# Second mixer and end of a fused block: constants computed early, sums in one piece, a remainder moved, the last gate in smaller steps

## What is computed

```
for i in range(2):                       # layer 0: short convolution, layer 1: RG-LRU
    h = h + mixer_i(rmsnorm(h, norm_mix[i]))
    h = h + hier_moe(rmsnorm(h, norm_ffn[i]), ...)          # 32 experts, top 2
    gate = sigmoid(rmsnorm(h, norm_ple[i]) @ w_ple_gate[i] + b_ple_gate[i])
    h = h + gate * (p[i] @ w_ple[i])
return rmsnorm(h, norm_final)

def rglru_mixer(xn):                     # the second mixer
    y, u = split(xn @ w_in)              # in_y and in_b below
    u = depthwise_conv(u, conv_w) + conv_bias               # width 4
    r, i = sigmoid(u @ w_r + b_r), sigmoid(u @ w_i + b_i)   # "gates", blocks of 256, two directions
    log_a = -8 * r * softplus(-lam)      # softplus(-lam): the decay constants
    a = exp(log_a)
    h = scan(a, sqrt(-expm1(2 * log_a)) * i * u)            # forward, and backward
    return (gelu(y) * (h_forward + h_backward)) @ w_out
```

## Time and profile before

| | |
|---|---|
| median of 3 runs | 1695.89 us (1693.95 to 1697.94) |
| profiled execution | 1695.1 us, its span 1693.1 us |
| TensorE busy | 1364.1 us (81%) |
| VectorE busy | 590.7 us (35%) |
| ScalarE busy | 434.9 us (26%) |
| HBM | 525.91 MB read, 311 GB/s over the span |

### The profile page before, as it was taken

How to read it: one execution, slowest core, us unless ns; L and a number is a source line. 1 busy time by engine, 2 the same in 40 slices (tenths; PEclk the granted TensorE clock), 3 DMA queues, 4 the chain that set the end, 5 groups by cost and what they waited for, 6 DMA issues and landing times.

```text
span 1693.1 us, 21874 instructions
## 1 busy us (share of the span) xinstructions
PE 1364.1 (81%) x9534; PEld 899.0 (53%) x9534; DVE 590.7 (35%) x1136; ACT 434.9 (26%) x658; POOL 219.7 (13%) x119
## 2 busy tenths in 40 slices
PE   4999998999999996776567677989966767666677
PEld 2797797999989961222122123978622212221226
DVE  2576623899437620110110012677201001101115
ACT  3444334534453320000000002566200000000015
POOL 0307322487430000000000000000000000000000
PEclk9999889999999997887888789999988878878789
DMA  9314435344554979999999999538799999999991
GB/s 403 122 61 166 196 111 201 120 179 153 171 199 156 393 318 429 427 426 427 427 429 427 427 425 412 211 110 358 275 427 427 427 426 428 427 427 427 426 411 71
DMA packets 51760, 528.39 MB, mean 312 GB/s; under 512 B 4688, under 2 KB 4816, under 8 KB 19920
## 3 DMA queue, kind: packets, MB, share of 16 engines
q1 hardware_dynamic: 51088, 525.22, 75.9%
q10 hardware_dynamic: 576, 1.75, 0.3%
HBM read 525.91 MB, written 1.05 MB: 311 GB/s over the span
## 4 chain that ended last, share of the span: by engine, by line
PE 50%; DMA 38%; DVE 5%; SPq 3%; ACT 2%; issue 1%; POOL 0%; DVEq 0%; ACTq 0%; POOLq 0%
PE bank L617 24%; PE bank L1180 9%; DMA ring<-in_w_up 7%; DMA ring<-in_w_gate 7%; DMA ring<-in_w_down 7%; DMA work<-in_w_gate 7%; DMA work<-in_w_up 4%; DMA work<-in_w_down 3%; PE bank L1200 3%; PE bank L1257 2%; SPq L518 2%; DMA ring<-in_dense 2%; PE bank L1326 2%; PE bank L610 1%; PE bank L689 1%; PE bank L1049 1%
## 5 line engine op out<-in xcount | busy, mean ns | idle before, releaser
L1180 PE MATMUL bank<-ring,work 128*32 128x512 f32 x1216 | 272.0, 731 | 141.4 <-DMA ring<-in_w_up 78.4
L617 PE MATMUL bank<-work_rounded,ring_rounded 128*128 128x256 f32 (+1 forms) x2032 | 317.5, 291 | 6.5 <-DVE xn_rounded L1940 3.5
L617 PEld LDWEIGHTS bank<-work_rounded,ring_rounded 128*128 128x128 f32 x2032 | 277.2, 190 | 16.1 <-issue 6.1
L617 PE MATMUL bank<-xn_rounded,ring_rounded 128*128 128x256 f32 (+1 forms) x1472 | 255.0, 291 | 3.4 <-DVE xn_rounded L1934 3.4
L1180 PEld LDWEIGHTS bank<-ring,work 128*32 128x32 f32 x1216 | 58.5, 130 | 319.6 <-issue 117.9
L617 PEld LDWEIGHTS bank<-xn_rounded,ring_rounded 128*128 128x128 f32 x1472 | 209.0, 194 | 7.7 <-issue 4.5
L2463 DVE TENSOR_TENSOR work<-work,bank 128x512 f32<-128x512 f32 x16 | 11.0, 687 | 569.5 <-PE bank L1180 569.5
L1835 POOL TENSOR_TENSOR ring_rounded<-ring,ring_rounded 128x2048 fp32r<-128x2048 f32 (+1 forms) x37 | 159.5, 4328 | 207.1 <-ACT ring_rounded L1394 207.1
L1180 PE MATMUL bank<-work 128*32 128x512 f32 x496 | 146.1, 698 | 33.6 <-DMA work<-in_w_gate 17.5
L1902 POOL TENSOR_TENSOR work<-work_rounded,work 128x128 f32<-128x128 f32 x32 | 12.1, 399 | 1079.2 <-PE bank L1232 738.4
L1394 ACT ACTIVATE ring_rounded<-ring 128x2048 fp32r<-128x2048 f32 (+1 forms) x78 | 136.5, 1795 | 46.3 <-PE bank L617 26.9
(11 more groups left out here) (329 smaller groups left out, 1718.0 us busy)
## 6 DMA issues: line engine op xcount, KB each, us to landing
ring<-in_dense SPq DMA_DIRECT2D x48, 2048.0 KB, 8.7
ring<-in_w_up SPq DMA_DIRECT2D x44, 2048.0 KB, 30.1
ring<-in_w_down SPq DMA_DIRECT2D x36, 2048.0 KB, 30.5
ring<-in_w_gate SPq DMA_DIRECT2D x32, 2048.0 KB, 29.8
work<-in_w_gate SPq DMA_DIRECT2D x16, 2048.0 KB, 23.1
work<-in_w_down SPq DMA_DIRECT2D x16, 2048.0 KB, 32.3
spare<-in_w_gate SPq DMA_DIRECT2D x8, 2048.0 KB, 28.9
work<-in_w_up SPq DMA_DIRECT2D x8, 2048.0 KB, 31.8
```

Of the source, the lines that this page charges most:

```text
L617: last = mm(out, rv(high_store[r][:, at:at + P]), rv(x[part][k]), start=opens and k == 0 and j == 0, stop=closes and k == n_k - 1 and j == 2)
L1180: ins = mm(out[slots(y), :], xg[:, k, slots(y)], expert_columns(w, at, 512), start=k == 0, stop=k == KT - 1)
```

## The change

1. The decay constants are computed at the start of the program, into a tensor of their own, with scratch in `small`.
2. In the second mixer the eight norm sums follow product k = 5 in one piece.
3. `weights_low(w_in_y)` for chunk 0 follows convolution block 3.
4. In the last layer the gate has five uses: three of two tiles, then tile 6 and tile 7 alone. VectorE prepares logits ahead; the last sums use a pairwise sum for tiles 0 to 3 and VectorE's square for tile 7; VectorE also scales tiles 5 to 7. The final multiply and store go in three parts (tiles 0 to 2, 3 to 5, 6 and 7).

```diff
+OUT_PARTS = ((0, 3), (3, 6), (6, 8))
-        ("out_b", 4), ("ple1", 4)]
+        ("out_b", 4), ("ple1", 5)]
+    rates = nc.alloc_sbuf_tensor("rates", [P, 16], F32)
+    def gate_tiles(layer, b):
+        return (2 * b, 2 * b + 2) if layer == 0 or b < 3 else (b + 3, b + 4)
-    nls = flat(17408, 16)
-    nlt = [flat(17424 + 16 * i, 16) for i in range(5)]
+    nls = rates[:]
+    nlt = [wk("small", 16, 16 * i) for i in range(5)]
...
@@ TensorE
             if k == 5:
-                sum_squares(range(4), h_sq)
-        sum_squares(range(4, KT), h_sq)
+                sum_squares(squared=h_sq)
...
-        sum_squares(squared=h_sq)
+        final = 4 * (count["norms"] + 1)
+        for k, sem, value in ((0, "sq_added", 3), (1, "sq_added", 3), (4, "sq_ready", final + 3), (5, "sq_ready", final + 3),
+                              (6, "sq_ready", final + 4), (7, "sq_added", 4)):
+            pe.wait_ge(S[sem], value)
+            last = mm(bank[4][:, 0:SEQ], ones, h_sq[:, k], start=k == 0, stop=k == KT - 1)
+        signal(last, "ss_ready")
@@ ScalarE, start
         high(w_abh, par("w_ab"))
+        act.wait_ge(S["lru_log"], 1)
+        signal(act.activation(nlt[1], nlt[1], ACT.Exp, scale=-1.0), "lru_exp")
@@ ScalarE, ple(1)
+            gate(0)
+            gate(1)
+            square(0)
+            normed(0, 1)
+            square(1)
+            gate(2)
+            normed(2, 3)
+            gate(3)
+            square(2)
+            square(3)
+            normed(4)
+            gate(4)
@@ ScalarE, second mixer
-        act.wait_ge(S["lru_log"], 1)
-        signal(act.activation(nlt[1], nlt[1], ACT.Exp, scale=-1.0), "lru_exp")
@@ VectorE, start
+        x = par("lam")
+        signal(v.scalar_tensor_tensor(nlt[1], x, -1.0, x, ALU.mult, ALU.max), "lru_log")
         low(par("w_ab"), w_abh, "dve_step")
+        dve.wait_ge(S["lru_exp"], 1)
+        log1p(nlt[2], nlt[1], nlt[3:5])
+        after(v.tensor_scalar(nlt[0], x, -1.0, 0.0, ALU.mult, ALU.max))
+        after(v.tensor_tensor(nlt[0], nlt[0], nlt[2], ALU.add))
+        signal(v.tensor_scalar(nls, nlt[0], -RG_C, None, ALU.mult), "lru_log")
+        dve.wait_ge(S["lru_log"], 2)
@@ VectorE, ple(1)
+            logits(0)
+            logits(1)
+            added(0)
+            added(1)
+            logits(2)
+            dve.wait_ge(S["sq_ready"], 4 * (7 + 3 * layer) + 2)
+            signal(v.tensor_tensor(h_sq[:, 0:2], h_sq[:, 0:2], h_sq[:, 2:4], ALU.add), "sq_added")
+            added(2)
+            logits(3)
+            added(3)
+            logits(4)
+            added(4)
+            dve.wait_ge(S["h_ready"], count["h_ready"])
+            signal(v.tensor_tensor(h_sq[:, 7], hT[:, 7], hT[:, 7], ALU.mult), "sq_added")
+            for k in range(5, KT):
+                last = v.tensor_scalar(weighted[:, k], hT[:, k], par("norm_final", k, 1), None, ALU.mult)
+            after(last)
@@ VectorE, second mixer: the operations of the start are gone from here, and
-            if b == 2:
-                weights_low(FIRST["w_in_y"])
+        weights_low(FIRST["w_in_y"])
@@ VectorE, end
-        for half in range(2):
-            part = slice(4 * half, 4 * half + 4)
+        for a, e in OUT_PARTS:
```

More of the change, by code:

```diff
@@ L584, in _ @@
                 sp.dma_start(ring[SLOT[n]][:, a:b], t["dense"][seen][:, a:b]).then_inc(S[full], 16)
-        for half in range(2):
-            part = slice(4 * half, 4 * half + 4)
-            sp.wait_ge(S["fin_ready"], half + 1)
-            sp.dma_start(t["out"][:, part], yT[:, part]).then_inc(S["out_store"], 16)
-        sp.wait_ge(S["out_store"], 32)
+        for i, (a, e) in enumerate(OUT_PARTS):
+            sp.wait_ge(S["fin_ready"], i + 1)
+            sp.dma_start(t["out"][:, a:e], yT[:, a:e]).then_inc(S["out_store"], 16)
+        sp.wait_ge(S["out_store"], 16 * len(OUT_PARTS))
     @block.tensor
@@ L1283, in ple @@
             ready = next_input()
-            for b in range(2, 4):
-                dense_split(use + b, [(n + 1, (2 * b + i) % 4) for i in range(2)],
+            for b in range(2, 4 + layer):
+                dense_split(use + b, [(n + 1, j % 4) for j in range(*gate_tiles(layer, b))],
                             [[x[:, k] for k in range(KT)] for x in (ple_xh, xnT)], None if b > 2 else ready)
@@ L1743, in ple, with gate, square, normed @@
             functions(SIGMOID)
-            for b in range(4):
+            def gate(b):
                 released(act, USE[f"ple{layer}"] + b)
-                for x in range(2):
-                    j = 2 * b + x
+                for j in range(*gate_tiles(layer, b)):
                     last = act.activation(gsb[:, j], gsb[:, j], ACT.Sigmoid, bias=par("b_ple", 8 * layer + j, 1))
                 signal(last, "gate_ready")
-                pair = slice(2 * b, 2 * b + 2)
+            def square(b):
                 act.wait_ge(S["h_ready"], 16 + 4 * layer + b + 1)
-                if layer == 0:
+                tiles = slice(*gate_tiles(layer, b))
+                signal(act.activation(h_sq[:, tiles], hT[:, tiles], ACT.Square), "sq_ready")
+            def normed(*tiles):
+                for k in tiles:
+                    act.activation(weighted[:, k], hT[:, k], ACT.Identity, scale=par("norm_final", k, 1))
+            if layer == 0:
+                for b in range(4):
+                    gate(b)
+                    act.wait_ge(S["h_ready"], 16 + b + 1)
                     for k in (2 * b, 2 * b + 1):
                         signal(act.activation(in_b_x[:, k], hT[:, k], ACT.Identity, scale=par("norm_mix", 8 + k, 1)), "emb_ready")
[L1755 to L1760, removed]
+                    square(b)
+                    if b in (1, 2):
+                        split_half()
+                return
+            gate(0)
[10 more added lines that the diff above has]
+            gate(4)
         moe(0)
@@ L2492, in ple, with logits @@
             roots()
-            for b in range(4):
+            def logits(b):
                 n = USE[f"ple{layer}"] + b
                 x = full(n)
-                pair = slice(2 * b, 2 * b + 2)
-                g = gsb[:, pair]
-                free(v.tensor_tensor(g, x[:].rearrange("p (k t) -> p k t", k=2), rstd_sb.unsqueeze(1).to_broadcast([P, 2, SEQ]), ALU.mult), n)
-                dve.wait_ge(S["gate_ready"], 8 * layer + b + 1)
[L2500 to L2503, removed]
+                a, e = gate_tiles(layer, b)
+                free(v.tensor_tensor(gsb[:, a:e], x[:, 0:SEQ * (e - a)].rearrange("p (k t) -> p k t", k=e - a),
+                                     rstd_sb.unsqueeze(1).to_broadcast([P, e - a, SEQ]), ALU.mult), n)
@@ new lines, in added @@
+            def added(b):
+                a, e = gate_tiles(layer, b)
+                g = gsb[:, a:e]
+                dve.wait_ge(S["gate_ready"], 8 * layer + b + 1)
+                after(v.tensor_tensor(g, g, ple_y(layer, a // 2)[:, a % 2:a % 2 + e - a], ALU.mult))
+                signal(v.tensor_tensor(hT[:, a:e], hT[:, a:e], g, ALU.add), "h_ready")
+            if layer == 0:
+                for b in range(4):
+                    logits(b)
+                    added(b)
+                    if b == 2:
+                        weights_low(FIRST["w_in_b"] + 1, (0,))
+                return
@@ L2505, in _ @@
+            for k in range(5, KT):
+                last = v.tensor_scalar(weighted[:, k], hT[:, k], par("norm_final", k, 1), None, ALU.mult)
+            after(last)
         moe(0)
         ple(0)
-        x = par("lam")
-        signal(v.scalar_tensor_tensor(nlt[1], x, -1.0, x, ALU.mult, ALU.max), "lru_log")
         weights_low(FIRST["w_in_b"] + 1, (1,))
@@ L2511, in _ @@
             weighted_low(weighted[:, k], hT[:, k], par("norm_mix", 8 + k, 1), weighted_high[:, k])
[L2513 to L2518, removed]
         def divided(out, n):
@@ L2597, in _ @@
         roots()
-        for half in range(2):
-            part = slice(4 * half, 4 * half + 4)
-            signal(v.tensor_tensor(yT[:, part], weighted[:, part], rstd_sb.unsqueeze(1).to_broadcast([P, 4, SEQ]), ALU.mult),
+        for a, e in OUT_PARTS:
+            signal(v.tensor_tensor(yT[:, a:e], weighted[:, a:e], rstd_sb.unsqueeze(1).to_broadcast([P, e - a, SEQ]), ALU.mult),
                    "fin_ready")
```

## The result

The changed kernel takes 1682.8 us (median of 4 runs, 1682.01 to 1683.07), the kernel before 1695.66 (4 runs, 1693.95 to 1697.94). The ratio is 0.992, 95% interval 0.9908 to 0.9932: 12.9 us less, as far as the medians go. The forecast was 1682.6. The profiled execution took 1682.87 us, its span 1680.9 (before 1695.1 and 1693.1).

The account below looks back on a forecast made before the run. VectorE's sequence from the second mixer's norm to `divided` b = 3 was taken as the bound. Gains 8.5 + 4.4 = 12.9 us from 1695.1 gave 1682.2, forecast 1682.6; own range 1680.6 to 1685, wider range 1679.6 to 1687.4.

Parts of the forecast that it names:

- The bound and the gap: Second mixer: VectorE's sequence from norm to `divided` b = 3 bounds; TensorE stands 6.6 us in line 610.
- Constants, sums, remainder: Second mixer: VectorE path loses 3.7 us of constants, 1.6 by sums, 4.40 of `weights_low`; lead beyond the wait not paid out.
- The clock: TensorE behind the mixer's gap: granted clock 0.53 for 3.62 us; the dip counted as 1.9 us.
- The 8.5: Second mixer's gain in us, last gate product 1129.78 to 1121.27; 6.6 if the clock dips anyway.
- The expert layer: Expert layer 1: its DMA stream moves with TensorE and VectorE and stays as long; first refill near 1207.4.
- The last gate: End of the kernel: logits ahead and single last tiles gain 4.4 us, bounds 3.0 and 5.0.
- the sooner first store: End of the kernel: first of three stores goes after three tiles, 0.95 against 1.23, gaining 0.3 us.
- The rules weighed: Last gate: two Trainium skill rules spoke against it, leaving an estimated 3.8 us (table switch) or 2.4 us (third store).
- The gap that stays: Rival, second mixer: gap of 1 to 2 us and clock dip return; mixer gives 5 us, time 1686; chance 0.10.
- The swallowed gain: Rival, expert layer: DMA stream swallows the mixer's gain, only 4.4 us left, time 1690.7; chance 0.06.
- the idle last gate: Rival, end of the kernel: last gate gives nothing because its ScalarE queue is longer, time 1686.6; chance 0.05.
- The slower one: Rival, TensorE from 1130 to 1227: unbroken stretch granted only clock 0.81, 22.8 us more, time 1705; chance 0.03.

Follow-up runs that it names:

- filler: The kernel before plus 14 TensorE products of no use between gate products 2 and 3; ratio to before 0.9989 (0.998 to 0.9998).
- low_only_filled: low_only plus four TensorE products of no use in its gap of 2.19 us; 1690.17 us, one run.
- low_back: The changed kernel with `weights_low(w_in_y)` back between convolution blocks 2 and 3; ratio to the kernel before 0.9941 (0.9927 to 0.9954).
- mixer_only: The kernel before with the constants, sums and remainder edits, and the old last gate; ratio to before 0.9954 (0.9942 to 0.9966).
- pairs: The changed kernel with the last gate in four uses of two tiles, logits still prepared ahead; ratio to the kernel before 0.9943 (0.9924 to 0.9961).
- low_only: The kernel before with only `weights_low(w_in_y)` moved behind convolution block 3; ratio to before 0.9972 (0.9962 to 0.9982).
- gap_longer: low_back plus one VectorE operation of no use ahead of the divide of block 3; 1688.92 us, one run.
- tail_only: The changed kernel without the constants, sums and remainder edits; ratio to the kernel before 0.9984 (0.9975 to 0.9993).

## Why the prediction was right

**The bound and the gap.** As put: line 610's wait for `divided` of block 3 was the price, and it is gone. Moved to the time of the kernel before (0.84 later), the first divide is at 1095.3 (predicted 1095.3), the fourth is done at 1109.5 (1109.5), the last gate function is at 1121.25 (1121.27).

**Constants, sums, remainder.** Each length was right, and so was the point that the surplus isn't paid out. (The constants are 16 operations of VectorE behind ScalarE's Exp, not 18; their 3.66 us are right.) What the sum left unsaid, the runs show: with the remainder moved, 2.2 us of idle time were left, and constants or sums alone remove them. Nothing is measurable in either once the other is in place. The load of the gelu weights was issued 1.7 us later behind the start of the sums (7.10 against 5.37), as forecast. Its rounding began 2.4 later (15.74 against 13.35), 0.6 more than the sum had, and cost nothing, since the bank that the first gate function frees was not wanted yet. `in_y0` did not wait.

**The clock.** The 8.5 held 1.9 us for it. Two kernels show it apart from the idle time (filler 1.66, low_only_filled 1.68); the rest of the 1.9 is the 0.3 that TensorE loses in taking up work, which low_back shows at a clock of 1.00. The term was right in size and held two costs under one name.

**The expert layer.** It moved with the mixer (mixer_only), and its refill went out at 1206.54, which is 1207.4 in the time of the kernel before, as predicted; the 1.0 us that it took longer in the profiled execution lies in its scatter.

**The last gate.** The term was 4.4: 4.2 up to the multiply, where 4.0 was measured, and 0.3 for the sooner first store, where -0.1 was measured. That last step was the wrong one. The first byte does move about 0.3 sooner behind the multiply (1.8 against 2.1), but the bytes take 0.1 longer (2.7 against 2.6) and 0.3 more pass behind the last one (1.2 against 0.9). Why the end behind the last byte is longer, no run settles. The missing 0.2 up to the multiply is spread thin: logits 0.46, sigmoid 0.54, TensorE's last sum 0.74 and the root 1.02, each to the start of the next step, where the prediction had 0.4, 0.5, 0.7 and 1.0; VectorE's product, addition and square took their 1.4. The three kinds of VectorE work listed there add up to 9.4, not 9.6, which changes nothing.

**The rules weighed.** For a switch of tables the Trainium skill ("ScalarE: Activation LUTs", section "What ACT_TABLE_LOAD costs") counts about 2.66 us, 1.28 for the load and 1.38 for a drain. The trace of pairs agrees on the load, 1.28, but the load starts right behind the activation before it and the next activation 0.01 us behind the load, so the measurement decides against the drain here. The Trainium skill ("DMA: Bandwidth & Descriptors", section "Anatomy of one DMA") gives a fixed 2.0 us for one DMA, measured for DMAs that GpSimd issues. The stores here are issued by SP, and a third one beside two others cost about 0.15.

**The rivals.** The gap that stays is low_only, at 4.4 us in place of 8.5, near the 5 that the prediction put on it. It had counted the clock's loss behind any gap of 1 to 2 us: gap_longer (2.06) bears that out, low_back (1.32) does not and keeps 6.9. The swallowed gain fell with mixer_only, the idle last gate with tail_only. The slower one needed a clock under 0.88 in the unbroken stretch: it was granted 1.00 from 1107.2 to 1217.

**The number.** That the forecast of 1682.6 lies 0.2 from the median is in part luck. The terms that the traces show add up to 8.5 + 4.0 - 0.1 = 12.4, not 12.9; the profiled pair differs by 12.2, the medians by 12.9, the ratio by 13.6 (11.5 to 15.6). The upper end of the forecast's own range was added up too low: 1.9 and 1.4 us above 1682.2 or 1682.6 give 1685.5 to 1685.9, not 1685.

## What to carry to other kernels

Work on a side engine is worth what it adds to the idle time of the engine that waits, so find when that engine asks, and stop there: here 9.7 us of lead were made where 6.6 counted, and either the constants or the sums could have been left as they were. Count the clock behind a gap of TensorE too, which can cost nearly as much as a short gap itself. In a serial end, prepare the next step's input ahead of the wait, and let the last step be the smallest tile that follows the last product; here the first, with the new order of the sums, gave 2.06 us and the second 1.94.

## What had not been expected

The clock falls behind some gaps and not behind others, and with the short ones it falls only after the gap. Behind 0.47, 0.55 and 1.32 us without work the granted clock stayed at 1.00. With 2.06 and 2.19 it was still 1.00 in the gap itself, and 0.62 and 0.53 in the 3.6 us after TensorE had taken up work again. In the 6.6 us of the kernel before it was 0.74 and behind them 0.53; behind the same 6.6 us in tail_only it was 0.61. So a gap of 2 us cost itself and 1.7 more. Each is one execution; no rule is drawn from them.
